# Three up projections of a gated feed-forward in seven block products for eight

## The reference

```python
def swiglu_ffn(x, w_gate_up, w_down):
    gu = x @ w_gate_up                       # 1024 -> 2 x 2816
    gate, up = gu[..., :FFN_HIDDEN], gu[..., FFN_HIDDEN:]
    return (jax.nn.silu(gate) * up) @ w_down # 2816 -> 1024

x = layer_norm(DN_ALPHA * x + swiglu_ffn(x, ffn_w_gate_up[i], ffn_w_down[i]), ln_g[i, 1], ln_b[i, 1])
```

## Time and profile before

| | us |
|---|---|
| median of 3 runs | 2246.77 |
| lowest, highest | 2246.28, 2247.21 |
| the profiled execution | 2248.02 |
| its span, first to last instruction | 2246.3 |
| TensorE busy | 2184.9 |
| VectorE busy | 1036.7 |
| ScalarE busy | 842.4 |
| GpSimd busy | 243.5 |

### The profile page before, as it was taken

How to read it: one execution, slowest core, us unless ns; L and a number is a source line. 1 busy time by engine, 2 the same in 40 slices (tenths; PEclk the granted TensorE clock), 3 DMA queues, 4 the chain that set the end, 5 groups by cost and what they waited for, 6 DMA issues and landing times.

```text
span 2246.3 us, 34926 instructions
## 1 busy us (share of the span) xinstructions
PE 2184.9 (97%) x14575; PEld 1791.7 (80%) x14575; DVE 1036.7 (46%) x1704; ACT 842.4 (38%) x1480; POOL 243.5 (11%) x327
## 2 busy tenths in 40 slices
PE   8999999999999999988999999999999999999998
PEld 7777778888888887867878888888976779888887
DVE  5243436454344345556547443333535555333335
ACT  5354444342232235234334323222446644222231
POOL 4000000000000011102314100000422214000000
PEclk9999999999999999989999999999999999999999
DMA  5312123233333323200013233333232212333321
GB/s 171 85 57 57 48 67 103 85 94 94 99 98 94 85 86 85 76 21 2 3 30 100 83 115 94 96 96 100 69 82 67 71 47 83 106 103 103 93 86 65
DMA packets 341336, 179.65 MB, mean 80 GB/s; under 512 B 44151, under 2 KB 332069, under 8 KB 341181
## 3 DMA queue, kind: packets, MB, share of 16 engines
q1 hardware_dynamic: 338860, 171.54, 27.2%
q0 software_dynamic: 2320, 5.89, 0.9%
HBM read 172.40 MB, written 2.11 MB: 78 GB/s over the span
## 4 chain that ended last, share of the span: by engine, by line
PE 45%; DVE 2%; POOL 1%; ACT 1%; issue 1%; DMA 0%; DVEq 0%; POOLq 0%; ACTq 0%
PE bank L462 13%; PE bank L464 13%; PE bank L463 13%; PE bank L1405 2%; PE bank L1431 1%; PE bank L1417 1%; POOL x L1063 0%; ACT w_hi L438 0%; PE bank L923 0%; PE bank L2933 0%; POOL act_lo L972 0%; PE bank L2941 0%; DVE w_lo L445 0%; DMA mla_swapped<-mla_qr 0%; DVE o L967 0%
## 5 line engine op out<-in xcount | busy, mean ns | idle before, releaser
L462 PE MATMUL bank<-act_hi,w_hi 128*128 128x512 f32 (+1 forms) x1960 | 737.0, 376 | 10.5 <-DVE w_lo L445 3.3
L464 PE MATMUL bank<-act_hi,w_lo 128*128 128x512 f32 (+1 forms) x1960 | 714.6, 365 | 0.0
L463 PE MATMUL bank<-act_lo,w_hi 128*128 128x512 f32 (+1 forms) x1960 | 714.4, 364 | 0.0
L445 DVE TENSOR_TENSOR w_lo<-w,w_hi 128x1024 fp32r<-128x1024 f32 (+2 forms) x327 | 400.2, 1225 | 404.5 <-ACT w_hi L438 404.3
L438 ACT ACTIVATE w_hi<-w 128x1024 fp32r<-128x1024 f32 (+1 forms) x328 | 336.6, 1028 | 342.2 <-PE bank L464 326.6
L462 PEld LDWEIGHTS bank<-act_hi,w_hi 128*128 128x128 f32 x1960 | 370.7, 189 | 84.2 <-issue 17.5
L464 PEld LDWEIGHTS bank<-act_hi,w_lo 128*128 128x128 f32 x1960 | 370.7, 189 | 60.1
L463 PEld LDWEIGHTS bank<-act_lo,w_hi 128*128 128x128 f32 x1960 | 371.4, 190 | 53.7 <-issue 1.0
L462 PE MATMUL bank<-hid_hi,w_hi 128*128 128x512 f32 (+1 forms) x672 | 249.5, 371 | 0.0
L463 PE MATMUL bank<-hid_lo,w_hi 128*128 128x512 f32 (+1 forms) x672 | 247.9, 369 | 0.0
L464 PE MATMUL bank<-hid_hi,w_lo 128*128 128x512 f32 (+1 forms) x672 | 247.8, 369 | 0.0
(11 more groups left out here) (440 smaller groups left out, 2352.4 us busy)
## 6 DMA issues: line engine op xcount, KB each, us to landing
w<-in_ffn_w_gate_up SPq DMA_DIRECT2D x88, 512.0 KB, 3.8
w<-in_w_in SPq DMA_DIRECT2D x41, 512.0 KB, 3.8
w<-in_w_up SPq DMA_DIRECT2D x32, 512.0 KB, 4.0
w<-in_w_down SPq DMA_DIRECT2D x32, 512.0 KB, 3.8
w<-in_ffn_w_down SPq DMA_DIRECT2D x32, 512.0 KB, 3.9
w<-in_even_w_in SPq DMA_DIRECT2D x28, 512.0 KB, 3.8
w<-in_ffn_w_down SPq DMA_DIRECT2D x16, 384.0 KB, 3.4
w<-in_w_out SPq DMA_DIRECT2D x8, 512.0 KB, 3.9
```

Of the source, the lines that this page charges most:

```text
L445: e.tensor_tensor(w_lo[:, 0:part.n], w.raw[part.g % w.LOADS][:, 0:part.n], w_hi[:, 0:part.n].bitcast(F32), ALU.subtract).then_inc(w.lo.sem, 1)
L462: e.matmul(s.acc, *first, start=(k == 0), stop=False)
L463: e.matmul(s.acc, *second, start=False, stop=False)
L464: last = e.matmul(s.acc, *third, start=False, stop=(k == kt - 1))
```

## The change

`up01`, `up02` and `up11` become `SevenJob`s. Two neighbouring tiles (gate and up, a pair) are a 2 x 2 block product: output tile x half of the features, by half of the features x half of the tokens. Winograd's form of Strassen's scheme makes its four result blocks with seven block products in place of eight, each of 4 k-tiles x 3 matmuls of 256 columns. For that

- sums of weights: four GpSimd additions of 512 values for each pair, from the raw tiles (`S`, in order s2, s1, s3, s4). Each pair has four parts, a (two raw blocks), b (s2, s1), c (s3, s4) and d (one raw block, 512 wide), each split in high part and remainder;
- sums of tokens: once for a layer, GpSimd rebuilds `x` from `AH` + `AL` and makes four sums for each of 4 k-tiles (`t`); ScalarE and VectorE split them behind four given tiles of the down job before the first seven-product chunk (`splits`);
- the results: `kept` (ScalarE) and z1 to z4 (VectorE) combine the products from four banks into `z` in SBUF, which `SiluTimes` then reads in place of a PSUM bank. In the text z1 is `z[:, 0:5:4]`, z2 `z[:, 5:7]`, z3 `z[:, 3]`, z4 `z[:, 1:3]`, and the seven products run in the order p1, p2, p6, p5, p7, p3, p4;
- loads and parts are counted apart: a pair has two loads and four parts. The raw slot of its first load is free when s4 and the remainder of a are made, that of the second when the remainder of d is;
- the rotary table starts behind `up00` + 5.

The core of the diff:

```diff
+    def add_pair(self, kt, first, second):
+        pair = Pair(self, self.pairs, [self.add_load(kt, pieces, P) for pieces in (first, second)])
...
+        pair.loads[0].freed = [self.sums.at(4 * pair.i + 4), self.lo.at(pair.parts[0].g + 1)]
+        pair.loads[1].freed = [self.lo.at(pair.parts[3].g + 1)]
...
+class SevenProducts(Hook):
...
+    def gpsimd(self, e):
...
+        for k in range(4):
...
+            for n in range(2):
+                e.tensor_tensor(self.y[:, n, :], core.AH[:, k + 4 * n, :].bitcast(F32), core.AL[:, k + 4 * n, :].bitcast(F32),
+                                ALU.add).then_inc(self.whole.sem, 1)
...
+            e.tensor_tensor(t1, b12, b11, ALU.subtract).then_inc(self.made.sem, 1)
+            e.tensor_tensor(t3, b22, b12, ALU.subtract).then_inc(self.made.sem, 1)
...
+            e.tensor_tensor(t2, b22, t1, ALU.subtract).then_inc(self.made.sem, 1)
...
+            e.tensor_tensor(t4, b21, t2, ALU.subtract).then_inc(self.made.sem, 1)
...
+        for s in self.subs:
...
+            if before:
+                e.wait_ge(*w.sums.at(4 * i))
+                e.wait_ge(*w.lo.at(before.parts[1].g + 1))
...
+            e.wait_ge(*w.landed_at(pair.loads[1]))
+            e.tensor_tensor(s1, a21, a22, ALU.add).then_inc(w.sums.sem, 1)
+            e.wait_ge(*w.landed_at(pair.loads[0]))
+            e.wait_ge(*w.sums.at(4 * i + 1))
+            e.tensor_tensor(s2, s1, a11, ALU.subtract).then_inc(w.sums.sem, 1)
+            if before:
+                e.wait_ge(*w.lo.at(before.parts[2].g + 1))
+            e.tensor_tensor(s3, a11, a21, ALU.subtract).then_inc(w.sums.sem, 1)
+            e.wait_ge(*w.sums.at(4 * i + 2))
+            e.tensor_tensor(s4, a12, s2, ALU.subtract).then_inc(w.sums.sem, 1)
...
+    def multiply(self, e, s, between):
...
+        if s is self.subs[0]:
+            e.wait_ge(*self.t_lo.at(4))
+        e.wait_ge(*w.lo.at(a.g + 1))
+        room(0)
+        product(p1, a, 0, plain(0, first)).then_inc(w.made.sem, 1)
+        room(1)
+        product(p2, a, 1, plain(1, first)).then_inc(w.used.sem, 1)
+        e.wait_ge(*w.lo.at(b.g + 1))
+        product(p6, b, 0, sums(1)).then_inc(w.made.sem, 1)
+        room(2)
+        product(p5, b, 1, sums(0)).then_inc(w.used.sem, 1)
+        e.wait_ge(*w.lo.at(c.g + 1))
+        product(p7, c, 0, sums(2)).then_inc(w.made.sem, 1)
+        room(3)
+        product(p3, c, 1, plain(1, second)).then_inc(w.used.sem, 1)
+        e.wait_ge(*w.lo.at(d.g + 1))
+        product(p4, d, 0, sums(3)).then_inc(w.used.sem, 1)
+
+    def emptied(self, i, n):
+        w = self.w
+        return (w.kept.at(i + 1), w.added.at(4 * i + 1), w.added.at(4 * i + 3), w.added.at(4 * i + 4))[n]
+
+    def scalar_pair(self, e, s):
...
+        e.activation(self.kept[:, :], self.halves(s.banks[0])[0], ACT.Copy).then_inc(w.kept.sem, 1)
+        for old in s.carried + s.pair.parts[0:2]:
+            for part in g.next_of(old):
+                g.split_high(e, part)
...
+    def vector_pair(self, e, s):
...
+        e.tensor_tensor(z[:, 0:5:4, :], p2_p6, spread(self.kept[:, :], 2), ALU.add).then_inc(w.added.sem, 1)
+        for old in s.carried + [a]:
+            for part in g.next_of(old):
+                g.split_low(e, part)
+        e.wait_ge(*w.made.at(3 * i + 3))
+        e.wait_ge(*w.added.at(4 * i + 1))
+        e.tensor_tensor(z[:, 5:7, :], p5_p7, spread(z[:, 4, :], 2), ALU.add).then_inc(w.added.sem, 1)
+        e.wait_ge(*w.added.at(4 * i + 2))
+        e.tensor_tensor(z[:, 3, :], p5_p7[:, 0, :], z[:, 6, :], ALU.add).then_inc(w.added.sem, 1)
+        for part in g.next_of(b):
+            g.split_low(e, part)
+        e.wait_ge(*w.used.at(d.g + 1))
+        e.tensor_tensor(z[:, 1:3, :], p3_p4, z[:, 5:7, :], ALU.add).then_inc(w.added.sem, 1)
...
+            if layer == 0 and c or layer and c == 1:
+                jobs[f"up{layer}{c}"] = SevenJob(w, f"up{layer}{c}", 2 * n, KD, pieces)
...
-    rope = Rope(core, ctx, A, values_at, g.start_of(J["up00"]) + 9)
+    rope = Rope(core, ctx, A, values_at, g.start_of(J["up00"]) + 5)
+    splits = [g.start_of(J["down00"]) + 3 + k for k in range(4)]
...
+    splits = [g.start_of(J["down10"]) + 2 + k for k in range(4)]
```

More of the change, by code:

```diff
@@ new lines, in raw_of, with landed_at, load @@
+    def raw_of(self, load):
+        return self.raw[load.n % self.LOADS]
+    def landed_at(self, load):
+        return self.landed[load.n % self.LOADS].sem, load.arrival
+    def load(self, e, n):
+        load = self.loads[n]
+        if n >= self.LOADS:
+            for freed in self.loads[n - self.LOADS].freed:
+                e.wait_ge(*freed)
+        for k0, kt, at, width, src in load.pieces:
+            t, col = divmod(at, load.width)
+            first = t * load.kt * load.width
+            dst = self.raw_of(load)[:, first:first + load.kt * load.width].rearrange("p (k n) -> p k n", n=load.width)
@@ L235, in load, with loads_before @@
                 dst = dst.rearrange("p k (h n) -> p (k h) n", n=src.shape[-1])
[L236 to L242, removed]
+            e.dma_start(dst, src).then_inc(self.landed[n % self.LOADS].sem, 16)
+    def loads_before(self, e, n):
+        n = min(n, len(self.loads))
+        for i in range(self.issued, n):
+            self.load(e, i)
+        self.issued = max(self.issued, n)
 class Job:
@@ L273, in factors, with __init__, bind_seven, starts @@
         return (w_hi[:, at:at + P], hi), (w_hi[:, at:at + P], lo), (w_lo[:, at:at + P], hi)
+class SevenJob(Job):
+    def __init__(self, weights, name, tiles, kt, pieces):
+        self.name, self.tiles, self.kt, self.group = name, tiles, kt, 1
+        self.pairs = [weights.add_pair(kt, pieces(u), pieces(u + 1)) for u in range(0, tiles, 2)]
+        self.parts = [part for pair in self.pairs for part in pair.parts]
+    def bind_seven(self, seven):
+        self.seven = seven
+        for pair in self.pairs:
+            pair.seven = seven
+    def starts(self, u, k):
+        return None
+    def ends(self, u, k):
+        return None
 class TokenJob(Job):
@@ L359, in __init__ @@
             s.n, s.acc, s.before = n, self.bank[b][:, s.cols], before.get(b)
-            before[b] = s
+            if s.pair is None:
+                before[b] = lambda s=s: s.job.epilogue.emptied(self, s)
+            elif s.group:
+                four = [(n + i) % self.BANKS for i in range(4)]
+                s.banks, s.befores = [self.bank[b] for b in four], [before.get(b) for b in four]
+                for i, b in enumerate(four):
+                    before[b] = lambda s=s, i=i: s.job.seven.emptied(s.pair.i, i)
             found[s.job, s.u, s.cols.start, s.cols.stop] = s
@@ L369, in __init__ @@
                         part.ended_in = leader.n + -(-leader.group * (k + 1) // s.job.kt) - 1
-            if not s.ends[-1]:
+            if s.pair and s.group:
+                s.last = n + 2 == len(self.subs) or self.subs[n + 2].pair is None
+                s.carried = self.subs[n - 1].pair.parts[2:] if self.subs[n - 1].pair else []
+                for k, part in enumerate(s.pair.parts):
+                    part.ended_by, part.ended_in = n + 1 if s.last and k >= 2 else None, None
+            elif not s.pair and not s.ends[-1]:
                 partial += 1
@@ L428, in replaced, with next_of @@
         return [(p, parts[p.g - self.SLOTS]) for p in parts[self.first + max(self.SLOTS, self.given):self.end]]
+    def next_of(self, part):
+        g = part.g + self.SLOTS
+        return [self.weights.parts[g]] if self.first + self.given <= g < self.end else []
     def first_parts(self):
@@ L444, in split_low @@
         w_hi, w_lo = self.split_of(part)
[L445 to L446 removed]
+        for at, src in part.sources():
+            last = e.tensor_tensor(w_lo[:, at], src, w_hi[:, at].bitcast(F32), ALU.subtract)
+        last.then_inc(w.lo.sem, 1)
     def multiply(self, e, group, between):
@@ L495, in _ @@
             for s in self.subs:
-                if s.group:
+                if s.pair and s.group:
+                    s.job.seven.multiply(e, s, between)
+                elif s.group:
                     self.multiply(e, self.subs[s.n:s.n + s.group], between)
@@ L517, in _ @@
                         self.split_high(e, part)
+                if s.pair and s.group:
+                    s.job.seven.scalar_pair(e, s)
                 s.job.epilogue.scalar(e, self, s)
@@ L543, in _ @@
                         self.split_low(e, part)
+                if s.pair and s.group:
+                    s.job.seven.vector_pair(e, s)
                 s.job.epilogue.vector(e, self, s)
```

199 lines of the change are left out of this document (168 added, 31 removed).

## The result

The changed kernel takes **2257.52 us** (median of 5 runs, 2256.97 to 2259.87) against 2247.21 for the kernel before (5 runs, 2246.28 to 2250.36): ratio **1.0046**, 95% interval 1.0032 to 1.0061. It is slower, by 10.3 us by the medians. The two profiled executions span 2255.7 and 2246.3 us, 9.4 apart. The forecast was 2254.5, +7.7.

A forecast was written before the change was run, and what follows sets the result against it. TensorE, busy 97% of the span, was taken as the bound. Chunks -0.3, edges +4.6 and +1.3, down stalls +2.1 gave +7.7 us on 2248.02: 2255.7, or 2254.5 as run median; own range 2248 to 2262, with rivals 2233 to 2266.

The forecast's parts named there:

- edge, even first product: Even layer's first product waits for split token sums, delayed by VectorE's load and three held additions: 4.6 us.
- edge, odd first product: Odd layer's first product waits for token-sum splits that stand a tile earlier: 1.3 us, bounds 0 to 4.6.
- three down stalls: Down tile after each changed chunk waits for the last hidden tile: 0.7 us three times, 2.1 us.
- TensorE's part: In the changed chunks, 84 matmuls of 256 columns take 10.07 us a pair against 10.88, saving 19.4 us for 24 pairs.
- Rival D: Switching operands between products slows 256-column matmuls to 129.5 ns, so TensorE gains nothing: 2250 us, chance 2%.
- The hold-off: VectorE operations with both operands in SBUF and GpSimd additions exclude each other, holding an addition about 1.16 us.
- the landing: Time from issue of a pair's second load to its data being there: 3.7 us, about 3.8 in the loop.
- The walk: Steps from one second-load landing to the next: 11.4 us a pair, third pair near 10.8, chunk 86.9 us.
- VectorE's own loop: VectorE's queue in a pair, 9.4 us plus about 2.0 of waiting, gives the same 11.4 us.
- rival C: Later landing, deciding once past 4.3 us, plus TensorE restarts: 12.0 us a pair, +9 us, edges 6, total 2265, chance 10%.
- Edges 3 and 4: Token sums on GpSimd under the first up chunk, and the rotary table started four tiles sooner: nothing each.
- Rivals A and B: Additions slip into gaps, pairs 10.07 us, total 2230.6, 16%; or two of four hold, about 10.7, total 2242, 12%.

The follow-up runs named there:

- run 1: Changed kernel with the four weight sums of every pair left out, GpSimd writing constants and reading nothing: 2228.20 us, ratio 0.9913.
- run 5: Changed kernel with silu's result and the gated product of the three chunks put in two idle PSUM banks, not SBUF: 2247.93 us, ratio 1.0001.
- run 7: On top of run 5, two more raw slots in the SBUF space it freed, so second loads go out earlier: 2229.79 us, ratio 0.9923.
- run 9: Changed kernel with the second load of pairs three to eight of each changed chunk halved to 256 KB: 2247.47 us, ratio 1.0003.
- run 6: Changed kernel with the split of the part behind b, in a chunk's last pair, moved behind the epilogue: 2252.83 us, ratio 1.0023.
- run 10: Kernel before the change with only the rotary table's steps moved four tiles sooner: 2248.09 us, ratio 1.0000.

## Why the prediction was right, and where its terms were off

```
us, against the kernel before       forecast   measured, by
TensorE, 24 pairs                    -19.4     -21.8  (run 1: 3 x 7.25)
waiting in the chunks                +19.1     +28.7  (chunks after less chunks of run 1)
edge, even first product              +4.6      +0.7  (0.89 between starts for 0.23)
edge, odd first product               +1.3       0.0
three down stalls                     +2.1      +2.7  (1.08, 1.24, 1.08 for 0.23)
elsewhere                              0        -1.0  (rest)
sum                                   +7.7      +9.4  (spans)
```
**TensorE's part** was right in kind, 2.4 us too small. A 256-column matmul is 118.7 ns from start to start in run 1 (79.79/672), 119.9 in the earlier trace rows, and a pair is 84 x 0.1187 = 9.97 for the 10.07 forecast. Rival D is out. The Trainium skill, *TensorE: Matmul & The Clock Gate*, "Back-to-back issue gap", gives N/2.4 + 2.5 ns for an isolated matmul, 109 ns at 256 columns; the trace does not agree, and the measurement stands.

**The hold-off** was right, and with the loop it is the cause of the 29 us. Run 1 takes the additions' reads away and all of it goes; run 5 leaves every addition in place, takes two holds away, and 9.6 us go; run 7 keeps the other holds, opens the loop over the load, and 18 more go. An estimate says that the loop needs the holds: four additions at 1.29 us, as s1 to s3 run in 5, would end about 5.4 us behind the landing, and with a landing of 4.07 the loop would close at 9.5 us, under TensorE's 9.97. No run has all four additions and no hold.

**The walk** was right in order and in length: 7.6 us behind the landing forecast, 7.72 measured. It called VectorE's own loop, 9.4 + about 2.0 of waiting, a second ground for 11.4. As a sum that holds, 9.1 + 2.3 in the pair of 11.45. But it is no second ground, since the landing sets how long VectorE is held: 2.3 us there, 3.0 in the pair of 12.11, and 1.9 in run 9 with the early landing, where this loop closes at 11.0.

**The mis-sized term in the chunks is the landing.** The forecast took 3.7 to 3.8 from the median of the earlier trace rows, for a load that goes out alone. The second of two came at 3.73 to 4.42, mean 4.07, so pairs four to seven took 11.79 and not 11.4 (+1.6 a chunk). And the third pair was not "near 10.8": its loads go out 1.1 us apart, the second lands after 4.4 to 4.9, and it took 11.95 (+1.15). With 0.4 back from the first two and the last pair, that is 2.3 a chunk, 7.0 in all. (The forecast's own pairs, 2 x 10.07 + 10.8 + 4 x 11.4 + 10.5, add up to 87.04 and not to the 86.9 that it wrote, so its -0.3 in all should have been 0.) It is rival C's mechanism, with 7.0 of its +9 us in the chunks. The price was right (0.1 us of landing is 0.1 us of pair) and the threshold of 4.3 was not, since there is none.

**The edges**, the two first products, were over-sized by 5.2 us, and this hid most of that. The step that failed is the size of a split of token sums. The forecast gave a quarter 2048 columns, 2.3 us on VectorE and 2.1 on ScalarE; a quarter is 4 x 256 = 1024, and takes 1.21 and 1.05. So a tile of 4.08 us held 0.69 + 1.23 + 1.21 = 3.1 us of VectorE's work and not 4.2. The three late additions are there: three of the four splits were held, the last one like this:
```profile
1321.58 2.32 DVE L895 TENSOR_TENSOR seven_t_lo<-seven_t,seven_t_hi 128x1024 fp32r<-128x1024 f32 x1
```
Most of that went into the slack; the first product came 0.66 late. In the odd layer it was not late at all. The down stall is 0.9 us each, 0.7 forecast, its cause as forecast: a remainder ahead of z4 (run 6). Edges 3 and 4 cost nothing, as said; 4 is shown by run 10, 3 only by the page, where the idle time ahead of the first matmul of a tile (L462 before, L579 after) is 10.5 us in both.

The total was close by luck: two errors of 5 and 7 us had opposite signs. The mechanism doesn't rest on that, but the size does. With the edges as measured (0.7 and 2.7) and the rest as forecast, the sum would have been +3.1, less than the 4.5 us that the forecast itself called indistinguishable from none. Of its signs of being right, the gap of some us before the first product did not show, and the pairs were 11.45 to 12.14 apart from the third on for the 11.2 to 11.7 named. One of its signs of being wrong would have misled: in the chunks TensorE's idle time was never ended by a DMA, and yet a load stood in the loop. It shows one engine further back, in GpSimd's first additions (37.5 us idle in up01, ended by the load). Rivals A and B were that the pair stays near 10 to 10.7; it does, once the load is out of the loop and two operands are out of SBUF (run 7), and this change had neither.

What is open: why the second of two loads 2.3 us apart lands now after 3.75 and now after 4.4; and the -1.0 us elsewhere, which is within what the profiled executions of two nearly equal kernels differ by (2246.3 and 2247.9 in run 10).

## What to carry to other kernels

Draw the loop before summing busy times: an arrival, the work that waits for it, and the release that lets the next one be issued. If a transfer stands in such a loop, its whole landing counts, with the spread that it has behind another load and not the median of a lone one; more buffers can be worth more than shorter work in the loop (here two raw slots gave 18 us of 2248, two holds less 9.6). Work moved to GpSimd, if it reads SBUF beside VectorE work with two SBUF operands, is not moved but interleaved: give one operand to PSUM, or keep the holds inside a slack.

## What the runs showed of the hardware

A GpSimd addition of 128x512 and a VectorE operation with two SBUF operands alternate without overlap: 1.22 us became 2.31, 0.69 became 1.79, and 1.29 became 1.75 the other way round. One PSUM operand on VectorE's side ended it (run 5: 0.70 beside an addition of 1.30). A 512 KB load that goes out 1.1 us behind another lands after 4.4 to 5.0 us, one 2.3 us behind after 3.7 to 4.4; at 256 KB these are 3.5 to 3.7 and 2.7 to 3.1. Halving the bytes (run 9) takes off 1.0 to 1.3 us of about 4. A stream of 256-column matmuls runs at 118.7 ns each over whole chunks at the full granted clock (run 1), 12 ns above 256 columns at 2.4 GHz.
